# The mLSTM score and decay products of a two-block kernel, from 64 and 4 rows to 128 padded rows

## What is computed

```python
qk = jax.nn.silu(_causal_conv(jnp.concatenate([mq, mk], axis=-1), ml_conv_w, ml_conv_b))
mq, mk = jnp.split(qk, 2, axis=-1)
h_ml = _mlstm(_to_heads(mq, ML_HEADS), _to_heads(mk, ML_HEADS), _to_heads(mv, ML_HEADS), ...)
# in _mlstm, per head; bcum is the running sum of log sigmoid(f), itil the input gate
logd = bcum[..., :, None] - bcum[..., None, :] + itil[..., None, :]
logd = jnp.where(causal, logd, -jnp.inf)
m_j = jnp.maximum(m_inter, logd.max(-1))
smat = jnp.einsum('bhcjd,bhcsd->bhcjs', qc, kc) * jnp.exp(logd - m_j[..., None])
```

## Time and profile before

| | us |
|---|---|
| median of 3 executions | 2509.34 |
| lowest, highest | 2507.38, 2515.93 |
| the profiled execution | 2507.15 |
| its span in the trace | 2505.3 |
| TensorE busy | 2070.7 (83%) |
| VectorE busy | 1729.9 (69%) |
| GpSimd busy | 1031.4 (41%) |
| mean granted clock of TensorE | 0.905 of full speed |

### The profile page before, as it was taken

One profiled execution on the slowest core, in us unless ns is written; L12 is line 12 of the kernel. 1 busy time (PEld: TensorE's weight loads), 2 busy tenths in 40 slices (PEclk: granted clock), 3 DMA queues, 4 the chain that ended last, 5 costly groups with the idle time before them and its releaser, 6 DMA issues. The chain is left out here.

```text
span 2505.3 us, 25385 instructions
## 1 busy us (share of the span) xinstructions
PE 2070.7 (83%) x7625; PEld 1307.4 (52%) x7625; DVE 1729.9 (69%) x3556; ACT 604.7 (24%) x1397; POOL 1031.4 (41%) x1083
## 2 busy tenths in 40 slices
PE   4985766889786986777889878887969797999999
PEld 4963544545342443343544433433449664788887
DVE  4856526999987876777767788888747553545464
ACT  2124312343232221122212232322121321101121
POOL 0001013667776776776766677777720000000000
PEclk9996787999988998898999998889989877999999
DMA  4751016999999999999999999999964101233322
GB/s 172 272 200 67 18 57 243 376 396 387 409 408 403 375 404 397 406 405 404 390 403 403 404 405 387 377 407 397 409 226 134 71 1 58 77 100 85 83 84 100
DMA packets 263737, 676.48 MB, mean 270 GB/s; under 512 B 22605, under 2 KB 111042, under 8 KB 263618
## 3 DMA queue, kind: packets, MB, share of 16 engines
q0 software_dynamic: 147456, 536.94, 54.7%
q1 hardware_dynamic: 116162, 138.13, 16.5%
HBM read 672.87 MB, written 2.10 MB: 269 GB/s over the span
## 5 line engine op out<-in xcount | busy, mean ns | idle before, releaser
L2201 PE MATMUL bank<-arena 128*128 128x512 f32 x1536 | 800.5, 654 | 171.9 <-DMA arena<-in_peer_v,arena 147.5
L2432 DVE SCALAR_TENSOR_TENSOR arena<-arena,h_ps 128x1024 f32<-128x1024 f32 x512 | 614.9, 1217 | 172.8 <-DMA arena<-in_peer_u,arena 165.1
L2164 POOL DMA_INDIRECT arena<-in_peer_v,arena x512 | 504.0, 984 | 249.1 <-issue 128.6
L2164 POOL DMA_INDIRECT arena<-in_peer_u,arena x512 | 512.2, 1000 | 227.5 <-issue 131.9
L2201 PEld LDWEIGHTS bank<-arena 128*128 128x128 f32 x1536 | 295.3, 206 | 520.8 <-issue 270.9
L2445 DVE SCALAR_TENSOR_TENSOR x<-arena,x 128x1024 f32<-128x1024 f32 x128 | 164.7, 1287 | 42.8 <-DMA arena<-in_peer_v,arena 31.0
L2286 ACT ACTIVATE arena<-ident,arena 128x128 f32<-128x128 f32 x384 | 135.9, 393 | 55.2 <-PE bank L2201 34.4
L142 DVE CAST parts<-arena 128x2048 fp32r<-128x2048 f32 (+4 forms) x60 | 68.1, 1136 | 112.5 <-DMA arena<-in_w_gate_up 72.1
L1453 PE MATMUL bank<-hT,arena 128*128 128x256 f32 x512 | 122.8, 397 | 18.6 <-DMA arena<-in_peer_w_q 17.2
L144 DVE TENSOR_TENSOR parts<-arena,parts 128x2048 fp32r<-128x2048 f32 (+4 forms) x60 | 126.7, 2111 | 4.5
L1453 PEld LDWEIGHTS bank<-hT,arena 128*128 128x128 f32 x512 | 102.1, 200 | 45.7 <-DMA arena<-in_peer_w_q 18.6
(11 more groups left out here) (414 smaller groups left out, 3335.5 us busy)
## 6 DMA issues: line engine op xcount, KB each, us to landing
arena<-in_w_ada SPq DMA_DIRECT2D x12, 2048.0 KB, 9.8
arena<-in_w_in SPq DMA_DIRECT2D x15, 1536.0 KB, 6.6
arena<-in_w_gate_up SPq DMA_DIRECT2D x44, 512.0 KB, 4.9
arena<-in_peer_w_q SPq DMA_DIRECT2D x16, 1024.0 KB, 16.2
arena<-in_w_down SPq DMA_DIRECT2D x22, 512.0 KB, 3.5
arena<-in_peer_u,arena POOLq DMA_INDIRECT x512, 8.8
arena<-in_peer_v,arena POOLq DMA_INDIRECT x512, 8.5
arena<-in_w_in SPq DMA_DIRECT2D x7, 1024.0 KB, 8.8
```

Source lines behind the costliest of these rows:

```text
L2164: nc.gpsimd.indirect_dma_start(out=ring[:, n % R, :], out_offset=None, in_=a[table][0], in_offset=bass.IndirectOffsetOnAxis(ap=expert[:, s ...
L2201: ins = nc.tensor.matmul(psum[half][:, :], diag[:, m % R, :], v_ring[:, n % R, half * 512:(half + 1) * 512], start=(s % PH == 0 and j == 0 ...
L2432: nc.vector.scalar_tensor_tensor(out=u_ring[:, n % R, :], in0=u_ring[:, n % R, :], scalar=1.0, in1=h_ps[:, :], op0=ALU.mult, op1=ALU.mult, ...
```

## The change

The queries of the mLSTM heads get a buffer of 128 partitions for each of the four heads, with zeros in the half that another head's channels would fill, and the score product takes all 128 partitions of queries and of keys. The decay product takes all 128 partitions of a gate buffer that is zeroed first, with a column of the full identity as the stationary operand. The row product of half A's softmax heads does the same. For that, four memsets are added: VectorE zeroes the queries of A in the gather stretch, GpSimd the gate rows of A there and the gate rows and queries of B in the norm of B. `silu` writes the queries in two instructions, one per half of the partitions, after a wait on `conv_padded`.

```diff
-        conv_q_of = [view(Y2 + 3072, 2, GT), view(17920, 2, GT)]
+        conv_q_of = [view(W_Q + 6 * GT + 1036 + ML_W, ML_H, GT), rows[:, 1, :].rearrange("p (h t) -> p h t", t=GT)]
...
         def silu(act, g):
             act.wait_ge(conv_summed, 4 * g + 4)
             act.preload_act_table_set("silu_and_others")
-            for half, o in enumerate((conv_q_of[g], conv_k[:, :, g * GT:(g + 1) * GT])):
-                ins = nc.scalar.activation(o, conv_out_of[g][:, 2 * half:2 * half + 2, :], ACT.Silu)
-            ins.then_inc(conv_ready, 1)
+            act.wait_ge(conv_padded, g + 1)
+            for side in range(2):
+                r = slice(side * HD, (side + 1) * HD)
+                nc.scalar.activation(conv_q_of[g].rearrange("p (j s) t -> p s j t", s=2)[r, side], conv_out_of[g][r, 0:2, :], ACT.Silu)
+            nc.scalar.activation(conv_k[:, :, g * GT:(g + 1) * GT], conv_out_of[g][:, 2:4, :], ACT.Silu).then_inc(conv_ready, 1)
...
-                j, r = (h - SM_H) // 2, slice((h - SM_H) % 2 * HD, (h - SM_H) % 2 * HD + HD)
...
-                nc.tensor.matmul(s, conv_q_of[p.g][r, j, t], conv_k[r, j, 0:n], start=True, stop=True)
+                nc.tensor.matmul(s, conv_q_of[p.g][:, h - SM_H, t], conv_k[:, (h - SM_H) // 2, 0:n], start=True, stop=True)
                 o, m = p.decay_ps[u % 2][:, 0:n], MF + h - SM_H
-                nc.tensor.matmul(o, ident[MF:MF + ML_H, m:m + 1].to_broadcast([ML_H, P]), gate_of[p.g].bias[MF:MF + ML_H, 0:n],
+                nc.tensor.matmul(o, ident[:, m:m + 1].to_broadcast([P, P]), gate_of[p.g].bias[:, 0:n],
                                  start=True, stop=False)
...
-                    nc.tensor.matmul(s, ident[0:SM_H, h:h + 1].to_broadcast([SM_H, P]), gate_of[p.g].bias[0:SM_H, 0:n],
+                    nc.tensor.matmul(s, ident[:, h:h + 1].to_broadcast([P, P]), gate_of[p.g].bias[:, 0:n],
...
             if slot == I0 + 7 * KD:
                 dve.wait_ge(sc_copied, 2 * PH)
+                dve.wait_ge(sc_summed, 2 * PH)
+                nc.vector.memset(conv_q_of[0], 0.0).then_inc(conv_padded, 1)
...
                             pool.wait_ge(sc_summed, 2 * PH)
+                            nc.gpsimd.memset(gate_of[0].bias, 0.0)
+                            pool.drain()
                             nc.gpsimd.iota(gate_of[0].bias[0:SM_H, :], [[1, GT]], base=0, channel_multiplier=0,
...
         def zero_gates(pool):
             nc.gpsimd.memset(view(raw_at[0], KD, 2 * NG), 0.0).then_inc(gates_zeroed, 1)
+            nc.gpsimd.memset(gate_of[1].bias, 0.0)
+            nc.gpsimd.memset(conv_q_of[1], 0.0).then_inc(conv_padded, 1)
             pool.drain()
```

More of the change, by code:

```diff
@@ L1484, in program @@
         log_f, m_i = view(PROJ_SB + 6656, T), view(PROJ_SB + 7168, T)
-        conv_q_of = [view(Y2 + 3072, 2, GT), view(17920, 2, GT)]
+        conv_q_of = [view(W_Q + 6 * GT + 1036 + ML_W, ML_H, GT), rows[:, 1, :].rearrange("p (h t) -> p h t", t=GT)]
+        assert W_Q + 6 * GT + 1036 + ML_W + ML_H * GT <= TK
         SMALL2 = Y2 + 3584
@@ L1551, in program @@
         row_moved, ones_ready = sem("row_moved"), sem("ones_ready")
+        conv_padded = sem("conv_padded")
         def load_w_2(sync, t):
```

## The result

| | before | after |
|---|---|---|
| median, us (5 executions of each) | 2507.38 | 2490.95 |
| lowest, highest, us | 2502.46, 2515.93 | 2484.72, 2492.91 |
| ratio after / before, 95% interval | | 0.9928, 0.9908 to 0.9948 |
| profiled execution, its span, us | 2507.15, 2505.3 | 2484.72, 2482.9 |
| mean granted clock | 0.905 | 0.921 |

By the ratio the changed kernel is 18 us faster, 13 to 23 by its interval; the ratio is not that of the medians, which differ by 16.4 us. The profiled executions differ by 22.4 us; the one of after is the lowest of its five. In after the lines have moved: the mLSTM score is L1834, the decay L1836, the mask L1853, the transposes of the probabilities L1895, VectorE's copy L1902 and the value sum L1916; the output product is L1737 and L1746.

The account below looks back on a forecast made before the run. TensorE, busy without gaps at a falling clock in half B's mLSTM heads, sets the pace there. Gains of 18.8 + 2.3 + 1.0 = 22.1 us lead to 2487 us; the forecast's own range is 2480 to 2494, eight-in-ten range 2480 to 2506.

Parts of the forecast that it names:

- Products: Half B's mLSTM heads: padded score and decay products take 0.64 us (384 columns) and 0.86 (512); decay bounds 0.64 to 0.84.
- 0.20 goes with the smaller row count itself.: A 64-row score product at 2.4 GHz takes 0.84 us for 384 columns, a 65-row one 0.64; row count costs the difference.
- VectorE next: Half B's mLSTM heads: TensorE's value sum waits for VectorE's copy, 0.6 us a pair, three waits, pair 6.1 us.
- The tail: Behind half B's last mask, 10.5 us before: TensorE's pieces at full clock gain 2.3 us, bounds 1.5 and 3.5.
- The output product: Stage after half B's attention: starts at a higher clock if it stays up, gaining 1.0 us, bounds 0 and 2.1.
- The sum: Total gain of 22.1 us: 18.8 from first mLSTM score to last mask, 2.3 behind it, 1.0 in the output product.
- Additions: Added memsets in gather stretch and half B's norm, and split query silu: all hidden, 0 us, bounds 0 and 4.2.
- half A: First half of the second attention, beside the gathers: shorter TensorE products count nothing as DMA is full; gain 0 to 2 us.
- Rival 1: Half B's mLSTM heads: zero rows leave the clock low; only the small form's extra 4.4 us is saved, 2505; chance 0.15.
- rival 2: Half B: the clock holds only partly, dropping in waits or tail; gain 11 to 12 us, 2498; chance 0.10.
- rival 3: Gather stretch and following norm: uncovered additions exceed savings, up to 4.2 us slower, 2513; chance 0.04.
- The rule against the change: Half B's odd heads: products in distinct row groups overlap, so full rows would lose 7.2 us; counted as nothing, chance one in a hundred.

Follow-up runs that it names:

- 64/64: Changed kernel with both mLSTM products, score and decay, at 64 rows instead of 128: median 2487.27 us, ratio to before 0.9925.
- the three later traces: Traces of the changed kernel run again (2583.08 us, slower chip), with padding in half B alone (2490.60), and with all-zero stationary operands (2490.22).
- The fillers: Changed kernel plus unused identity-by-ones products in half B: five before its first softmax score, four in waits behind the last mask; 2482.27 us, ratio 0.9903.

## Why the prediction was right, step by step

**The time.** 2487 was predicted; 2490.95 was measured, inside the forecast's own range. The gain was forecast at 22.1 us and measured at 16.4 by the medians, 18 by the ratio. The prediction started from a median of 2509.34; over five executions it is 2507.38, from which the sum gives 2485.3, 5.7 too low. So the time came out closer than the gain. The mechanism was the one named: TensorE sets the pace in the mLSTM heads, and at 1.00 of the clock the stretch is half as long. "22.6 us against 41.4" was 21.66; 18.8 us of gain were 19.7.

**Products.** The padded ones took 0.65 (384 columns), as taken from the 65-row products; the padded decay, for which no row stood, lies at the lower end of its bounds.

**"0.20 goes with the smaller row count itself."** The size was right and the reason wrong: the cost follows the neighbours, 0.1 us for each of another form. With 64/64 a product has one such neighbour and takes 0.75 or 0.74, and in distinct halves two cost 0.85 together.

**VectorE next.** I took three waits of 0.6 us, 1.8 in all. Two were to be seen, of 0.25 and 0.30, and a pair took 5.47 to 5.93 instead of 6.1. That is 1.25 us less than I took, more than the 0.9 us by which the stretch was shorter than my sum. The step behind it was the reading that the 3.50 us from the mask to the end of the copy are nearly all ScalarE and VectorE. VectorE's store in before, then the store and the copy behind it in after:

```profile
2060.56 0.16 DVE L1921 SCALAR_TENSOR_TENSOR arena<-arena 128x1 f32<-128x1 f32 x1 [0.29 <-PE h_ps L1913]
```

```profile
2038.50 0.15 DVE L1924 SCALAR_TENSOR_TENSOR arena<-arena 128x1 f32<-128x1 f32 x1
2039.41 0.55 DVE L1902 COPY arena<-h_ps 128x384 f32<-128x384 f32 x1
```

In before the store waits 0.29 us for TensorE's value sum, which ran at half clock; in after there is no such wait, and from the mask (2036.91) to the end of the copy (2039.41 + 0.55) it is 3.05 us. So 0.45 us of the 3.50 were TensorE's own low clock, in the value sum and in the mask product itself (0.29 us long in before, 0.22 in after).

**The tail.** Behind the last mask I took 2.3 us, and it was 0.7 (1.05 in the three later traces), under its lower bound of 1.5. The step that failed is that the pieces of TensorE there would keep the clock: in 2050 to 2060 us it is busy 5.69 of 10 us and the clock 0.63. The output product, 1.0 in my sum, gained nothing (3.12 against 3.10) for the same reason. The fillers show that the gain I had looked for there exists: with the clock at 1.00 the tail is 8.60 us, 1.9 less than in before, and in all 4.3 us are gained behind the first mLSTM score once TensorE isn't left idle.

**The sum.** 22.1 against 22.4 in the spans is luck in part: the tail and the output product were 2.6 too high, the stretch 0.9 too low, and 2.0 us of the traced gain are the gather stretch's scatter. Against the 20.4 us behind the first mLSTM score the sum was 1.7 too high, against 17.6, the lower end of the traces, 4.5, and against the measured 16 to 18 us 4 to 6.

**Additions, half A.** The four additions took 0.91, 0.34, 0.53 + 0.96 and 0.63 us each against 0.95, 0.26, 1.5 and 0.62. Those of half B were hidden. Of those in the gather stretch no run shows a cost or its absence, since B's norm starts anywhere within 13 us there. Half A brought nothing that can be measured, as counted.

**Rivals.** Rival 1 (zeros leave the clock low) is refuted by after itself and by the kernel with all-zero stationary operands, rival 2 by 1.00 in every window of the stretch, rival 3 by the time. **The rule against the change** I had dismissed as not borne out. It does hold, for products in one form: the change gave up 0.44 or 0.66 us in each of the odd heads' four units against the 64/64 form. The prediction's 7.2 us were lengths at half clock; at 1.00 it is 2.2 us in all. But the kernel before didn't have that overlap, so against before nothing was lost.

## What to carry to other kernels

A TensorE that is busy all the time may still run at half its clock: read the granted clock by windows of one stage, and where it is low with small row counts in the products, enlarge the smaller of them with zero rows (64 were enough for the decay here, at the price of two memsets) before padding everything. Give neighbours the same row form, and put pairs of 64-row products into opposite halves, where they run side by side. Where TensorE waits just before a dense stage, useless products in the wait can pay more than they cost: here nine of them brought 8 us.

## What the hardware showed that I had not expected

- The granted clock fell to a mean of 0.56 over 41 us in which TensorE had no gap (64-row and 4-row products), and was 1.00 throughout with 64 and 32, 64 and 64, 64 and 128, 128 and 4 rows, or with 128 rows and all-zero stationary operands.
- Two 64-row products in opposite halves start 0.01 us apart and take 0.85 us together for 384 columns in float32 (1.06 for 512); 64 beside 32 or 4 rows never overlapped.
- A product costs about 0.1 us more for each neighbour of another row form (0.65, 0.74 and 0.84 us for 384 columns with none, one and two).
- Products without use made a stretch shorter by 10 us (30.40 against 40.21), and in other places the whole kernel by 8 us (2482.27 against 2490.60).
